# Two blocks on one NeuronCore: weight parts of the seven-product blocks prepared one product earlier, and the first FFN's input placed 448 bytes further on

## The chip, the cores and the metric

The kernel runs on one core of a Trainium2 chip. Its time is the device time of one execution in microseconds (us). A program on the core is split over five engines with a queue of instructions each: TensorE (PE, matrix products), VectorE (DVE), ScalarE (ACT), GpSimd (POOL), and SyncE (SP), which here only issues DMAs. Each queue runs in its own order and waits on semaphores for the others.

## The reference

Two transformer blocks follow each other on x of 512 tokens by 1024 features, all in float32. Only their feed-forward parts (FFN) matter here:

```
hffn = modulate(rmsnorm(x, g_norm2[l]), shift2, scale2)
a, u = jnp.split(jnp.einsum('bsd,df->bsf', hffn, w_ffn_in[l]), 2, axis=-1)
x = x + gate2[:, None, :] * jnp.einsum('bsf,fd->bsd', jax.nn.silu(a) * u, w_ffn_out[l])
...
h = rmsnorm_2(x, norm_ffn[l])
x = x + (jax.nn.silu(h @ w_ffn_gate[l]) * (h @ w_ffn_up[l])) @ w_ffn_down[l]
```

The hidden width is 2816, which is 22 tiles of 128. The rest (an adaptive norm, stick-breaking attention, retention, sparse attention with a learned index, gated linear attention) is the same in both kernels.

## The kernel before

Activations lie with features on the partitions and the 512 tokens along the row. Every float32 operand is split into a high part, rounded to `fp32r`, and a low part (the rest), and a product of tiles is three matmuls, high by high, low weight by high, high weight by low (L1800, L1802, L1805, 512 columns each). Weights come in blocks of 1024 by 256 into one of three buffers `stg` (SP), ScalarE rounds the high part into `wh`, and VectorE or GpSimd subtracts it for the low part `wl`. There are six slots of 128 by 512 in each of `wh` and `wl`.

Both FFNs ("a" is the first, "b" the second) compute most of their gate and up columns in another way, which saves an eighth of the products: a weight block (2 by 2 halves) and the input (2 by 2 halves) are multiplied in seven products instead of eight, with sums of the parts as operands (the method of Strassen and Winograd). A product `(g, m)` is product m of block g. It is 12 matmuls of 256 columns, four times L1830 (high by high), L1832 (low weight `wl`) and L1834 (low input). Products 1, 2 and 3 read the input itself, `hH`/`hL` in FFN a and `h2H`/`h2L` in FFN b; products 4 to 7 read sums of it, `tHa`/`tLa` and `tHb`/`tLb`. Each FFN does this in two lots of ten blocks, gate and up in turn, with the products onto the output width behind each lot. Before the first lot's blocks stand four ordinary jobs of 512 columns on the same input (96 matmuls in all).

The weights of products 1, 2 and 4 are corners of the block, straight from `stg`; their low parts are made by GpSimd (L3086). Those of products 3, 5, 6, 7 are sums of corners, S4, S1, S2, S3, which VectorE writes into PSUM (L2321; S1, named `bank<-stg`, reads two corners in SBUF, S4 is `bank<-stg,bank_pair`, S3 `bank_pair<-stg,bank_pair`, S2 `bank_pair<-bank,stg`), and their low parts VectorE makes too (L2327). ScalarE makes all high parts (L2828) in the order of the products. After a product, `part` adds it to what belongs to it: VectorE after products 1, 6 and 7 (L2343), ScalarE after 2, 3 and 5 (L2840). After product 4 and product 6 a finished row of the block is multiplied, put through silu, split (`row_mult`, `row_silu`, `row_scale`, `row_high`, `row_low`): VectorE L2353/L2355 or L2359/L2361 and L2089, GpSimd L3095, L3099, L3110, L3021. FFN b scales both blocks' rows by the norm's factor, so GpSimd has eleven operations in 14 products there, and eight in FFN a.

The order of products is the list `items`. In the steady state, with block g and the next one n, it is (n,5), (g,6), (n,2), (n,3), (g,7), (n,1), (g,4). `fast` writes out every engine's order around it: before product i, `before(i)` first emits the low parts whose high parts the last call emitted (`lows`), then the sums that are due and whose places are free, and then prepares the next items as far as a limit on `state["next"]` allows, where `quad_high` is emitted and the low part is left for the next call. After the product come its `part` and the row steps that are due. A slot can be written once the product six slots back is done. A block's `stg` buffer is loaded anew when its last low part (product 4) and last sum are done. Whatever the code emits, each engine runs it in that order.

Of the kernel before, what the change touches and what calls it, by code (L numbers as in the profile page):

```python
# [9 lines left out]
F32R = mybir.dt.float32r  # L10
# [3 lines left out]
P = 128  # L14
S = 512
D = 1024
KT = D // P
# [269 lines left out]
def make_plan():  # L287
    p = Plan()
# [412 lines left out]
    def ffn(tag, x, wa, wu, u0, wd, lo):  # L701
# [65 lines left out]
        def fast(lot, groups, lead, tail):  # L767
# [19 lines left out]
            state = {"next": 1, "open": False}  # L787
# [36 lines left out]
            def before(i):  # L824

                while lows:
                    low(*lows.pop(0))
                due.extend(sums.get(i, ()))
                while due and ready(*due[0]):
                    add(*due.pop(0))  # L830
                while state["next"] < len(items):
                    item = items[state["next"]]
                    if isinstance(item, int) and item < p.ahead:
                        state["next"] += 1
                        continue
                    if isinstance(item, int):
                        u = len(p.units) + len(p.units) % 2
                        if state["next"] > i + 3 or not (p.done(u - 6) and p.done(u - 5)):
                            return
                        p.prepare(item)  # L840
                    else:
                        g, m = item
                        if state["next"] > i + (4 if i < len(lead) and not lot else 3 if m in (1, 2, 4, 5) else 2) or not p.done(len(p.units) - 6):
                            return
                        if m in (3, 5, 6, 7) and (g, {5: 1, 6: 2, 7: 3, 3: 4}[m]) not in p.summed:
                            return
                        for b in range(p.groups[g]["b"], p.groups[g]["b"] + 3):
                            p.load(b)
                        p.quads[g, m] = {"u": len(p.units)}
                        p.units.append(("quad", g, m))  # L850
                        p.n_hi += 1
                        p.quads[g, m]["hi"] = p.n_hi
                        emit("quad_high", g, m)
                        lows.append((g, m))
                    state["next"] += 1
# [75 lines left out]
        for lot, (f0, nf) in enumerate(((0, FA), (FA, FT - FA))):  # L931
# [24 lines left out]
            if groups:  # L956
                start = last - len(groups) - 2
                lead = [start, start + 1]
# [392 lines left out]
def program(nc, a, out, scratch):  # L1351
    p = make_plan()
# [4 lines left out]
    def sb(name, shape, dt=F32, ctx=base):  # L1357
        return ctx.enter_context(nc.sbuf_tensor(name, shape, dt))

    with base:  # L1360
# [15 lines left out]
        small = sb("small", [P, 320])  # L1376
        sb("place_h", [P, 16])
        XR = sb("XR", [P, KT, S])
        hH = sb("hH", [P, KT, S], F32R)
        hL = sb("hL", [P, KT, S], F32R)  # L1380
        SQ = sb("SQ", [P, S])
        MEAN = {n: matf[:, i, :] for i, n in enumerate((D, 512, P))}
        RT = SQ
# [113 lines left out]
        def operand(x, k):  # L1497

            what = x[0] if isinstance(x, tuple) else x
            if what == "os":  # L1500
                return osH[:, k, :], osL[:, k, :]
            if x == ("or", 3):
                return or3H[:, k, :], or3L[:, k, :]
            if what == "or":
                return orH[:, k, :], orL[:, k, :]
            if what == "h4" and k >= 4:
                return goH[:, k - 4, :], goL[:, k - 4, :]
            if what == "mg":
                return mH[:, k, :], mL[:, k, :]
            if what == "h5":  # L1510
                return h2H[:, k, :], h2L[:, k, :]
            if what == "fa":
                return fHa[:, k, :], fLa[:, k, :]
            if what == "fb" and k >= KT:
                return fHb[:, k - KT, :], fLb[:, k - KT, :]
            return hH[:, k, :], hL[:, k, :]
# [1685 lines left out]
```

## Time and profile before

| | |
|---|---|
| median of 3 runs | 1801.43 us (1801.07 to 1806.17) |
| the profiled execution | 1803.78 us, of which 1802.0 us from the first to the last instruction (span) |
| mean granted TensorE clock | 0.997 |
| FFN a, product blocks | from about 841 to 939 us, and 1005 to 1107 us |
| FFN b, product blocks | from 1464 to 1562 us, and 1627 to 1731 us |

The profile is of one execution. In its timeline a row is one instruction (or a run of like ones): start, duration, engine, line, what it writes and reads. TensorE's matmuls overlap: one lasts 0.28 us, and the next begins 0.11 to 0.12 us after it, so the time of a product is the distance between the first matmul of it and that of the next. A wait can therefore hide in a matmul that lasts longer, and the idle time of PE is less than what a late operand costs.

### The profile page before, as it was taken

The numbers are of one execution on the slowest core, as the hardware profiler recorded it, in microseconds if no ns is written. First come the engines' busy times: TensorE is split into PE (matmuls) and PEld (weight loads), VectorE is DVE, ScalarE is ACT, GpSimd is POOL, SyncE is SP. The second block draws the span as 40 slices with busy tenths as digits, with TensorE's granted clock in tenths as the row PEclk, the third lists the DMA queues.
The fourth block names the chain that finished last, engine by engine and source line by source line (L and its number), as shares of the span: only waits on it lengthen the run. The fifth ranks groups of instructions, "written<-read, shape, count | busy, mean of one in ns | idle before, by whom it ended". The sixth has DMA issues, their size and how long they took to land.

```text
span 1802.0 us, 25394 instructions
## 1 busy us (share of the span) xinstructions
PE 1774.3 (98%) x9960; PEld 1468.2 (81%) x9960; DVE 962.6 (53%) x1600; ACT 804.8 (45%) x1355; POOL 794.7 (44%) x607
## 2 busy tenths in 40 slices
PE   9999999999999999999999999999999999999997
PEld 7777778878778787887998899777776789888986
DVE  7567541434151303338764465648777677635754
ACT  5555551233233323437552354535546565424542
POOL 5444345546365534432540243144556347505740
PEclk9999999999999999999999999999999999999999
DMA  9321223545443122422533233432222123232322
GB/s 355 119 70 48 71 71 116 177 147 174 147 140 105 60 93 71 140 94 73 152 95 116 72 117 97 116 98 83 92 80 76 47 71 111 93 125 71 114 92 76
DMA packets 158872, 192.12 MB, mean 107 GB/s; under 512 B 10345, under 2 KB 141689, under 8 KB 158370
## 3 DMA queue, kind: packets, MB, share of 16 engines
q1 hardware_dynamic: 156898, 181.77, 31.2%
q0 software_dynamic: 1104, 5.24, 0.9%
q10 hardware_dynamic: 752, 3.49, 0.5%
q8 instruction: 80, 1.31, 0.3%
q14 instruction: 38, 0.31, 0.1%
HBM read 188.37 MB, written 4.72 MB: 107 GB/s over the span
## 4 chain that ended last, share of the span: by engine, by line
PE 91%; DVE 6%; issue 2%; ACT 1%; DMA 0%; POOL 0%; DVEq 0%; ACTq 0%
PE bank L1800 19%; PE bank L1805 19%; PE bank L1802 19%; PE bank L1832 6%; PE bank L1834 6%; PE bank L1830 6%; PE bank L1909 2%; DVE wl L2327 1%; PE bank L1843 1%; PE bank_pair L1805 1%; PE bank_pair L1802 1%; PE bank_pair L1800 1%; PE bank_pair L1859 1%; DVE left L2164 1%; PE bank L1879 1%
## 5 line engine op out<-in xcount | busy, mean ns | idle before, releaser
L1800 PE MATMUL bank<-hH,wh 128*128 128x512 f32 x1040 | 424.8, 408 | 0.0
L3030 POOL TENSOR_TENSOR wl<-stg,wh 128x512 fp32r<-128x512 f32 x150 | 202.6, 1351 | 475.1 <-ACT wh L2639 474.9
L1805 PE MATMUL bank<-hL,wh 128*128 128x512 f32 x1040 | 406.4, 391 | 0.0
L1802 PE MATMUL bank<-hH,wl 128*128 128x512 f32 x1040 | 405.8, 390 | 0.0
L2639 ACT ACTIVATE wh<-stg 128x1024 fp32r<-128x1024 f32 (+2 forms) x222 | 216.6, 978 | 217.4 <-PE bank L1805 168.4
L3086 POOL TENSOR_TENSOR wl<-stg,wh 128x512 fp32r<-128x512 f32 x120 | 165.7, 1390 | 196.0 <-ACT wh L2828 195.7
L1800 PEld LDWEIGHTS bank<-hH,wh 128*128 128x128 f32 x1040 | 195.4, 188 | 56.6 <-issue 19.7
L1805 PEld LDWEIGHTS bank<-hL,wh 128*128 128x128 f32 x1040 | 195.2, 188 | 42.3
L1802 PEld LDWEIGHTS bank<-hH,wl 128*128 128x128 f32 x1040 | 195.7, 188 | 39.3 <-issue 2.9
L3031 POOL TENSOR_TENSOR wl<-stg,wh 128x512 fp32r<-128x512 f32 x150 | 204.8, 1366 | 0.0
L2343 DVE TENSOR_TENSOR tmps<-bank,tmps 128x256 f32<-128x256 f32 x120 | 50.8, 424 | 111.0 <-PE bank L1834 111.0
L2840 ACT ACTIVATE tmps<-bank 128x256 f32<-128x256 f32 x120 | 45.9, 384 | 143.7 <-PE bank L1834 143.4
L2121 DVE TENSOR_TENSOR wl<-stg,wh 128x768 fp32r<-128x768 f32 (+2 forms) x72 | 75.9, 1060 | 61.8 <-ACT wh L2639 61.4
L2134 DVE CUSTOM_DVE_ANT_0 stg<-stg,cb,col 128x1024 f32<-128x1024 f32 x32 | 55.7, 1775 | 79.8 <-DMA stg<-in_w_ada_t 79.8
L1832 PE MATMUL bank<-tHb,wl 128*128 128x256 f32 x320 | 90.5, 283 | 2.5 <-DVE wl L2327 1.7
L1832 PE MATMUL bank<-tHa,wl 128*128 128x256 f32 x320 | 89.8, 281 | 2.2 <-DVE wl L2327 1.7
L1830 PE MATMUL bank<-tHb,wh 128*128 128x256 f32 x320 | 88.8, 278 | 2.2 <-DVE tmps L2343 2.2
L1830 PE MATMUL bank<-tHa,wh 128*128 128x256 f32 x320 | 89.1, 278 | 1.4 <-DVE tmps L2343 1.4
L1834 PE MATMUL bank<-tLa,wh 128*128 128x256 f32 x320 | 88.7, 277 | 0.0
L1834 PE MATMUL bank<-tLb,wh 128*128 128x256 f32 x320 | 88.7, 277 | 0.0
L2828 ACT ACTIVATE wh<-stg 128x512 fp32r<-128x512 f32 x120 | 75.7, 631 | 11.5 <-PE bank L1805 11.5
L1832 PE MATMUL bank<-hH,wl 128*128 128x256 f32 x240 | 68.4, 285 | 1.4 <-DVE wl L2327 1.4
(394 smaller groups left out, 4065.7 us busy)
## 6 DMA issues: line engine op xcount, KB each, us to landing
stg<-in_w_in SPq DMA_DIRECT2D x54, 1024.0 KB, 5.2
stg<-in_w_ada_t SPq DMA_DIRECT2D x48, 512.0 KB, 4.7
stg<-in_w_ffn_in SPq DMA_DIRECT2D x22, 1024.0 KB, 5.1
stg<-in_w_ffn_gate SPq DMA_DIRECT2D x11, 1024.0 KB, 5.3
stg<-in_w_ffn_up SPq DMA_DIRECT2D x11, 1024.0 KB, 5.4
stg<-in_w_proj_ret SPq DMA_DIRECT2D x8, 1024.0 KB, 5.1
stg<-in_w_out SPq DMA_DIRECT2D x8, 1024.0 KB, 5.6
stg<-in_w_ffn_out SPq DMA_DIRECT2D x8, 768.0 KB, 4.9
```

The lines of the kernel that those rows point to most:

```text
L1800: T.matmul(ps, wh, xh, start=j["first"] and k == 0, stop=False)
L1802: T.matmul(ps, wl, xh, start=False, stop=False)
L1805: t = T.matmul(ps, wh, xl, start=False, stop=j["stop"] and last)
L1830: T.matmul(ps, wh[:, k, :], xh, start=k == 0 and m in (1, 2, 5), stop=False, skip_group_check=True)
L1832: T.matmul(ps, wl[:, k, :], xh, start=False, stop=False, skip_group_check=True)
L1834: t = T.matmul(ps, wh[:, k, :], xl, start=False, stop=k == KT // 2 - 1, skip_group_check=True)
L2121: V.tensor_tensor(lo, src, hi, ALU.subtract).then_inc(s["w_lo_dve"], 1)
L2639: A_.activation(hi, src, ACTF.Copy).then_inc(s["w_hi"], 1)
L2828: A_.activation(hi, src, ACTF.Copy).then_inc(s["w_hi"], 1)
L3030: G.tensor_tensor(lo[:, 0:h, :], src[:, 0:h, :], hi[:, 0:h, :], ALU.subtract)
L3031: G.tensor_tensor(lo[:, h:, :], src[:, h:, :], hi[:, h:, :], ALU.subtract).then_inc(s["w_lo_pool"], 1)
L3086: G.tensor_tensor(lo, src, hi, ALU.subtract).then_inc(s["w_lo_pool"], 1)
```

## The change

Two edits. The first is in the limit on how far ahead items may be prepared: products 1, 2, 4, 5 at most four items ahead instead of three, products 3, 6, 7 three instead of two (four for all in the lead of a first lot, as before). When the sums are made doesn't change in the code.

The second makes `hH` and `hL` one allocation with 128 more columns. All users but one keep their addresses. The first FFN's input (`"hn2"`) is now written and read 112 columns, 448 bytes, further on. From `hH` at byte 103040 of a partition the input moves to 103488: 128 bytes past a multiple of 512 before, 64 bytes past one now, as `h2H` (138304), `tHa` (143424) and `tHb` (171072) were. Everything allocated behind moves by 512 bytes, and keeps its place relative to 512.

```diff
-                        if state["next"] > i + (4 if i < len(lead) and not lot else 3 if m in (1, 2, 4, 5) else 2) or not p.done(len(p.units) - 6):
+                        if state["next"] > i + (4 if m in (1, 2, 4, 5) or i < len(lead) and not lot else 3) or not p.done(len(p.units) - 6):
...
-        hH = sb("hH", [P, KT, S], F32R)
-        hL = sb("hL", [P, KT, S], F32R)
+        hHL = sb("hHL", [P, 2 * KT * S + 128], F32R)
+        hH, hL = (hHL[:, i * KT * S:(i + 1) * KT * S].rearrange("p (k s) -> p k s", k=KT) for i in range(2))
+        nH, nL = (hHL[:, i * KT * S + 112:(i + 1) * KT * S + 112].rearrange("p (k s) -> p k s", k=KT) for i in range(2))
...
+            if what == "hn2":
+                return nH[:, k, :], nL[:, k, :]
```

Lines behind the second edit have numbers higher by three in the changed kernel. TensorE's and SP's instructions keep their order. On VectorE in FFN b, from the `row_mult` of an up block on (gate block g, next block n), the kernel before has: the low part of (g,6), S4 of n, S3 of g, `part` after (g,6), `row_low`, the low parts of (n,3) and (g,7), S1 of the block after n, `part` after (g,7), and a low part of product 5:

```order
L2353 TENSOR_TENSOR tmps<-bank,tmps 128x256
L2355 TENSOR_TENSOR tmps<-tmps 128x256
L2327 TENSOR_TENSOR wl<-bank_pair,wh 128x512
L2321 TENSOR_TENSOR bank<-stg,bank_pair 128x512
L2321 TENSOR_TENSOR bank_pair<-stg,bank_pair 128x512
L2343 TENSOR_TENSOR tmps<-bank,tmps 128x256
L2089 TENSOR_TENSOR hL<-tmps,hH 128x512
L2327 TENSOR_TENSOR wl<-bank,wh 128x512
L2327 TENSOR_TENSOR wl<-bank_pair,wh 128x512
L2321 TENSOR_TENSOR bank<-stg 128x512
L2343 TENSOR_TENSOR tmps<-bank,tmps 128x256
L2327 TENSOR_TENSOR wl<-bank,wh 128x512
```

The same stretch of VectorE in the changed kernel:

```order
L2356 TENSOR_TENSOR tmps<-bank,tmps 128x256
L2358 TENSOR_TENSOR tmps<-tmps 128x256
L2324 TENSOR_TENSOR bank<-stg,bank_pair 128x512
L2330 TENSOR_TENSOR wl<-bank,wh 128x512
L2324 TENSOR_TENSOR bank_pair<-stg,bank_pair 128x512
L2346 TENSOR_TENSOR tmps<-bank,tmps 128x256
L2092 TENSOR_TENSOR hHL<-tmps,hHL 128x512
L2330 TENSOR_TENSOR wl<-bank_pair,wh 128x512
L2324 TENSOR_TENSOR bank<-stg 128x512
L2330 TENSOR_TENSOR wl<-bank,wh 128x512
L2346 TENSOR_TENSOR tmps<-bank,tmps 128x256 x2
L2330 TENSOR_TENSOR wl<-bank_pair,wh 128x512
```

The low part of (g,6) now stands ahead of the `row_mult` (out of sight here), that of (n,3) has moved from behind S3 and `row_low` to between S4 and S3, and that of the next product 5 from behind to ahead of the `part` after (g,7).

On GpSimd in FFN b, from one `row_low` (L3021) to the next, two blocks of the kernel before (L3099 is `row_mult` of the gate block, L3095 that of the up block, L3110 `row_scale`, L3086 low parts of products 2, 1, 4 in turn):

```order
L3021 TENSOR_TENSOR hL<-tmps,hH 128x512
L3086 TENSOR_TENSOR wl<-stg,wh 128x512
L3099 TENSOR_TENSOR tmps<-tmps,SQ 128x512
L3086 TENSOR_TENSOR wl<-stg,wh 128x512 x2
L3110 TENSOR_TENSOR tmps<-tmps,SQ 128x512
L3086 TENSOR_TENSOR wl<-stg,wh 128x512
L3110 TENSOR_TENSOR tmps<-tmps,SQ 128x512
L3095 TENSOR_TENSOR tmps<-tmps 128x512
L3086 TENSOR_TENSOR wl<-stg,wh 128x512 x2
L3021 TENSOR_TENSOR hL<-tmps,hH 128x512
```

And in the changed kernel:

```order
L3024 TENSOR_TENSOR hHL<-tmps,hHL 128x512
L3089 TENSOR_TENSOR wl<-stg,wh 128x512 x2
L3102 TENSOR_TENSOR tmps<-tmps,SQ 128x512
L3089 TENSOR_TENSOR wl<-stg,wh 128x512
L3113 TENSOR_TENSOR tmps<-tmps,SQ 128x512
L3089 TENSOR_TENSOR wl<-stg,wh 128x512
L3113 TENSOR_TENSOR tmps<-tmps,SQ 128x512
L3089 TENSOR_TENSOR wl<-stg,wh 128x512
L3098 TENSOR_TENSOR tmps<-tmps 128x512
L3089 TENSOR_TENSOR wl<-stg,wh 128x512
L3024 TENSOR_TENSOR hHL<-tmps,hHL 128x512
```

In both blocks the low part of the next block's product 1 has moved ahead of `row_mult`, which now stands between it and the low part of product 4. ScalarE's order moves in step: the high part of each product is emitted one product earlier, as far as its sum is there.

## Rows read from the trace of the kernel before

**Rows 1.** The page, busy time of each engine (share of the span), instructions.

```profile
PE 1774.3 (98%) x9960; PEld 1468.2 (81%) x9960; DVE 962.6 (53%) x1600; ACT 804.8 (45%) x1355; POOL 794.7 (44%) x607
```

**Rows 2.** Waits of PE: for whom, us in total, times, longest.

```profile
PE bank L1832 <- DVE wl L2327: 6.6, 20, 1.3
```

**Rows 3.** Groups of matmuls by form: count, then busy us, mean ns of one.

```profile
L1830 PE MATMUL bank<-hH,wh 128*128 128x256 f32 x240 | 67.6, 282 | 0.0
...
L1802 PE MATMUL bank<-h2H,wl 128*128 128x512 f32 x32 | 12.6, 395 | 0.0
...
L1802 PE MATMUL bank<-fHa,wl 128*128 128x512 f32 x132 | 51.4, 389 | 0.0
```

**Rows 4.** Timeline of PE, first matmuls of products, FFN a, then FFN b.

```profile
845.64 0.28 PE L1830 MATMUL bank<-hH,wh 128*128 128x256 f32 x1
...
847.08 0.29 PE L1830 MATMUL bank<-tHa,wh 128*128 128x256 f32 x1
...
1467.09 0.28 PE L1830 MATMUL bank<-h2H,wh 128*128 128x256 f32 x1
...
1468.45 0.28 PE L1830 MATMUL bank<-h2H,wh 128*128 128x256 f32 x1
```

**Rows 5.** Timeline of PE, FFN b, two blocks (24 gate, 25 up).

```profile
1506.70 0.28 PE L1830 MATMUL bank<-h2H,wh 128*128 128x256 f32 x1
...
1509.42 0.28 PE L1830 MATMUL bank<-tHb,wh 128*128 128x256 f32 x1
...
1510.78 0.28 PE L1830 MATMUL bank<-tHb,wh 128*128 128x256 f32 x1
1511.13 0.39 PE L1832 MATMUL bank<-tHb,wl 128*128 128x256 f32 x1
...
1519.84 0.28 PE L1830 MATMUL bank<-tHb,wh 128*128 128x256 f32 x1
...
1526.97 0.28 PE L1830 MATMUL bank<-h2H,wh 128*128 128x256 f32 x1
```

**Rows 6.** Timeline of VectorE in the same stretch.

```profile
1509.72 0.42 DVE L2353 TENSOR_TENSOR tmps<-bank,tmps 128x256 f32<-128x256 f32 x1 [0.43 <-PE bank L1834]
1510.06 0.42 DVE L2355 TENSOR_TENSOR tmps<-tmps 128x256 f32<-128x256 f32 x1
...
1510.99 0.69 DVE L2321 TENSOR_TENSOR bank<-stg,bank_pair 128x512 f32<-128x512 f32 x1
1511.59 0.69 DVE L2321 TENSOR_TENSOR bank_pair<-stg,bank_pair 128x512 f32<-128x512 f32 x1
1512.70 0.43 DVE L2343 TENSOR_TENSOR tmps<-bank,tmps 128x256 f32<-128x256 f32 x1 [0.42 <-PE bank L1834]
...
1514.84 1.83 DVE L2321 TENSOR_TENSOR bank<-stg 128x512 f32<-128x512 f32 x1
```

**Rows 7.** Timeline of ScalarE in the same stretch.

```profile
1512.31 0.60 ACT L2828 ACTIVATE wh<-bank_pair 128x512 fp32r<-128x512 f32 x1
1512.80 0.62 ACT L2828 ACTIVATE wh<-stg 128x512 fp32r<-128x512 f32 x1
```

**Rows 8.** Timeline of GpSimd in the same stretch.

```profile
1513.20 1.66 POOL L3099 TENSOR_TENSOR tmps<-tmps,SQ 128x512 f32<-128x512 f32 x1 [3.08 <-DVE tmps L2343]
1514.82 3.00 POOL L3086 TENSOR_TENSOR wl<-stg,wh 128x512 fp32r<-128x512 f32 x2
1517.78 1.30 POOL L3110 TENSOR_TENSOR tmps<-tmps,SQ 128x512 f32<-128x512 f32 x1
```

**Rows 9.** The page, DMA issues: count, KB, us from issue to landing.

```profile
stg<-in_w_ffn_gate SPq DMA_DIRECT2D x11, 1024.0 KB, 5.3
```

**Rows 10.** Timeline of PE, FFN a, two blocks: first matmuls 14 products apart.

```profile
883.41 0.28 PE L1830 MATMUL bank<-hH,wh 128*128 128x256 f32 x1
...
903.71 0.28 PE L1830 MATMUL bank<-hH,wh 128*128 128x256 f32 x1
```

**Rows 11.** Timeline of VectorE, FFN a, S1 of block 3.

```profile
863.29 3.15 DVE L2321 TENSOR_TENSOR bank<-stg 128x512 f32<-128x512 f32 x1 [1.89 <-DMA stg<-in_w_ffn_in]
```

## The prediction, as it went on record

> **What bounds the kernel now.** I read the page's busy shares first: PE is busy 98% of the span, VectorE 53%, ScalarE 45%, GpSimd 44% [rows 1]. So only PE's own time counts, or what makes PE late. The waits of PE say how late: 6.6 us in 20 waits for low parts from VectorE [rows 2]. That understates it, since a waiting matmul looks long. In the timeline of PE a product with its operands there takes 1.36 us (1467.09 to 1468.45); one on the first FFN's input takes 1.44 (845.64 to 847.08) [rows 4]. Against that two blocks of FFN b, fourteen products, take 20.27 us (1506.70 to 1526.97) [rows 5] where 14 x 1.36 is 19.04: 1.23 us are lost per pair of blocks. In FFN a a pair takes 20.30 [rows 10]; six of its products read the input at 0.08 more each, so 0.78 are lost. One loss is seen whole: product (24,6) begins at 1510.78 and its first `wl` matmul only at 1511.13, 0.35 later instead of 0.11 [rows 5].
>
> The cause is an order. The low part of (24,6) stands on VectorE behind the `row_mult` of block 23 (1509.72, 1510.06) [rows 6], which waits for product (23,4) to end at 1509.42 [rows 5]. The low part of the next product 3 stands likewise behind `part` and `row_low`.
>
> **Part 1, the placement.** 60 products of FFN a read the input (240 matmuls of one kind, four in a product [rows 3]). At 64 bytes past a multiple of 512 they should take the 1.36 us of `h2H`, which lies so, instead of 1.44 [rows 4]: 60 x 0.08 = 4.8 us less. The same place costs the ordinary 512-column jobs something: 395 ns on `h2H` against 389 on `fHa`, which lies 128 past [rows 3]; 96 x 6 ns = 0.6 more. Net -4.2 us. Bounds: 0, if the 0.08 belongs to something else about that input, and -4.8.
>
> The Trainium skill ("TensorE: Matmul & The Clock Gate", "Back-to-back issue gap") puts the gap at the columns over 2.4 GHz plus 2.5 ns, 109 ns at 256 columns as an estimate, whatever the address. The trace shows 113 and 120 on like matmuls at one clock [rows 4], and by the page alone part 1 would be worth 0.
>
> **Part 2, the order.** Nothing is added or removed; three things move. I take the end of product (g-1,4) as zero (1509.42 in the rows) and follow the gate block of a pair in FFN b, with durations from the three engines' timelines [rows 6 to 8]: a 512-wide VectorE operation holds its queue 0.60 and is done after 0.69, a 256-wide one 0.34 and 0.42; ScalarE 0.49 and 0.60; GpSimd 1.26 and 1.30 (1514.82 + 3.00 is 1517.82, the next begins at 1517.78). VectorE starts `row_mult` 0.30 after the product's end (1509.42 to 1509.72); other handovers I take as 0.04 to 0.08, as from 1512.70 + 0.43 to 1513.20.
>
> Before: `row_mult` 0.30, S4 at 1.57, S3 at 2.17 [rows 6], high part of (g,7) 2.89, of (n,1) 3.38 to 4.00 [rows 7]. GpSimd did `row_mult` at 3.78 (1.66 long), then the low parts of (n,1) and (g,4), 5.40 to 8.40 [rows 8]. (g,4) begins six products later, at 8.16 without a stall.
>
> After: the low part of (g,6) is long made, so PE's stalls there go (the gain). `row_mult` waits 0.08 for S2 and runs to 1.04; S4 1.04 to 1.73. Now the low part of (n,3) stands between S4 and S3, and needs its high part first: ScalarE 1.77 to 2.36, VectorE 2.40 to 3.08, VectorE idle for 0.75 in front of it. S3 thus runs 3.00 to 3.69 instead of 2.17 to 2.86. High part of (g,7) 3.73, of (n,1) 4.21 to 4.84. GpSimd has the low part of (n,1) first in its queue now, so it idles until 4.92 although `row_mult` could start at about 4.1, and is done at 6.21. VectorE meanwhile does `part` (3.60), `row_low` (3.95), the low part of (g,7) (4.55 to 5.23, PE wants it at 5.55: no stall), and comes to S1 of the block after n at 5.15.
>
> S1 reads two tensors in SBUF, and so does every GpSimd operation here. The rows show what happens when they meet [rows 6, 8]: S1 at 1514.84 took 1.83 us instead of 0.69 beside a GpSimd operation begun at 1514.82, and the two GpSimd operations took 3.00 together instead of 2.55. The Trainium skill ("SBUF — State Buffer", "SBUF: two separate sides") has this as an exclusive lock on a shared port pair, held for a whole instruction, against VectorE operations with two SBUF inputs; the trace agrees with these numbers.
>
> So S1 waits to 6.21 and ends at 6.77; GpSimd's `row_mult` runs from there to 8.06 and the low part of (g,4) to 9.33. PE gets it at 9.39 and wants it at 8.16 + 0.11 = 8.27: a stall of 1.12 and 0.11 for the restart (as where the matmul behind a stalled one is late too [rows 5]). The half pair lasts 10.75 us, where it lasted 10.42 (1509.42 to 1519.84) [rows 5].
>
> The up block's half goes the same way from its zero: `row_mult`'s second half meets a GpSimd low part (0.34 lost), S4 1.30 to 1.99, low part of product 3 to 3.34, S3 3.26 to 3.95, high part of product 1 to 5.10, GpSimd low part 5.18 to 6.46, S1 to 7.02, `row_mult` to 8.28, low part of product 4 to 9.58: PE is late by 1.37, the half lasts 11.0 where it lasted 20.27 - 10.42 = 9.85. With the same meeting in the next gate half (0.25) a pair takes 22.0: 1.7 more than before. Ten blocks are five pairs in a lot, the first one only partly in this state, so nine pairs in two lots: +15 us. None of the busy shares [rows 1] shows such a limit, since the engines of this chain take turns.
>
> FFN a has no `row_scale`, and `row_mult` on GpSimd for up blocks alone. Gate half: GpSimd's low part of (g,4) is done by 8.06, in time. But the low part of the next product 5 stands ahead of the `part` after (g,7): S1 ends 6.77, high part 7.41, low part begins 7.44, `part` 8.04 to 8.47, and product (g,4), which adds to that result, begins at 8.52 instead of 8.16. With the restart 0.47, up to 0.7 where `row_mult` met GpSimd. Up half 0.1 to 0.2. A pair loses about 0.9 instead of 0.78: +1 us over nine pairs. Bounds for it: -7 (nothing is late any more), +12 (below).
>
> SP's queue keeps its order; a `stg` load waits for the low part of product 4, at 9.33 behind zero, and takes 5.3 us [rows 9], so it lands at about 14.7. Its first reader is the S1 in the next half, at about 10.75 + 5.2 = 15.9: hidden, by 1.2 us. If that cover went, VectorE would stand still as it once did in FFN a [rows 11].
>
> **Sum.** -4.2 + 15 + 1 = +12 (11.8) on the profiled execution's 1803.8 us: 1815.6. That execution is 2.4 above the median of the three runs, so 1813 us in their terms.
>
> **Rivals.**
>
> *Faster: the stalls vanish and nothing replaces them.* For it: the only operands that PE waits for steadily are VectorE's low parts, and these do come earlier; no engine is near its limit. Then FFN b gives back 9 x 1.23 = 11 us, FFN a 9 x 0.78 = 7, with the placement 22: 1779. The deciding point is whether GpSimd's low part of product 4 is ready 8.2 us after zero. Against: even in the order before it was ready only at 8.40 (1517.82) [rows 8], and had slack only since PE had stalled earlier. If just one step of my chain failed, the meeting of S1 with GpSimd, the stall in the gate half would still be 0.6. Half of this rival lies near 1787. Chance 0.22.
>
> *Nothing but the placement counts.* The new stalls weigh as much as the old ones, in FFN b too: 1797 to 1807. It needs S3's delay of 0.8 us and GpSimd's new order to cost half of what I found. Chance 0.15.
>
> *Worse: S1 loses the port twice.* In one place S1 took 3.15 us [rows 11], since a second GpSimd operation went ahead of it. In FFN a that would put `part` after (g,7) another 1.3 us late in each pair, +12: 1825. Elsewhere it lost once only [rows 6]. Chance 0.07.
>
> *The placement gives nothing*, the rest as forecast: 1817, inside the forecast's own range.
>
> **How the numbers follow.** The forecast has a chance of 0.56, with its own range of 1807 to 1822 (FFN b from +9 to +20, FFN a from -1 to +4, placement -4.8 to 0). What 0.3% of this kernel is, 5.4 us, is about what a measurement tells from no change. Faster 0.22 (the first rival), same 0.15 (the second), slower 0.63 (forecast and double loss). The range of 1790 to 1822 leaves out the far part of the first rival (0.14) and the double loss (0.06).
>
> **What would show it.** The products on the first FFN's input 1.36 us apart. In FFN b first matmuls 14 products apart by 21.5 to 22 us; the stalls of products 6 and 3 gone, and in their place idle time of PE in front of the `wl` matmul of product 4, released by GpSimd's low part (L3089), twice per pair; S1 on VectorE (L2324) longer than 1 us in most pairs; VectorE idle before the low part of product 3, released by ScalarE. In FFN a short waits for the `part` after product 7. The forecast is wrong if GpSimd's low part of product 4 comes before PE: then a pair in FFN b would be shorter than 20.27.

## The result and the profile after

The changed kernel takes 1817.98 us (median of 4 runs, 1815.0 to 1819.78); the kernel before, run beside it, 1803.16 (4 runs). The ratio is 1.0075, with a 95% interval of 1.0063 to 1.0087: 11 to 16 us slower. The profiled execution has a span of 1816.6 us, 14.6 more than before. The page's busy shares (engine, us, share of the span, instructions) and its chain by engine:

```profile
PE 1779.4 (98%) x9960; PEld 1470.8 (81%) x9960; DVE 1000.4 (55%) x1600; ACT 805.1 (44%) x1355; POOL 795.2 (44%) x607
...
PE 80%; POOL 6%; DVE 6%; issue 5%; ACT 2%; DMA 0%; DVEq 0%; ACTq 0%; POOLq 0%
```

The shares hardly differ from those of before [rows 1]. VectorE is busy 38 us longer with the same 1600 instructions, so some of them got longer. The waits of PE (for whom; us in total, times, longest) show where it waits now:

```profile
PE bank L1833 <- DVE tmps L2346: 13.1, 20, 2.9
PE bank L1835 <- POOL wl L3089: 4.3, 14, 0.3
PE bank L1835 <- DVE wl L2330: 2.6, 2, 1.3
```

Of the kernel before, the second line of the view from which [rows 2] shows the first:

```profile
PE bank L1830 <- DVE tmps L2343: 3.7, 3, 1.4
```

The 20 waits for low parts from VectorE [rows 2] have become 2. The waits for `tmps`, which is the `part` behind product 7 that product 4 adds to, have grown from 3 to 20, and 14 for low parts from GpSimd are new. Timeline of PE in FFN b, at three products 4 and at the end of the first of them (start, us; in brackets the idle time before and its releaser):

```profile
1510.95 0.38 PE L1833 MATMUL bank<-tHb,wh 128*128 128x256 f32 x1 [0.43 <-DVE tmps L2346]
1511.64 0.38 PE L1835 MATMUL bank<-tHb,wl 128*128 128x256 f32 x1 [0.31 <-POOL wl L3089]
...
1513.02 0.28 PE L1833 MATMUL bank<-tHb,wh 128*128 128x256 f32 x1
...
1521.75 0.38 PE L1833 MATMUL bank<-tHb,wh 128*128 128x256 f32 x1 [0.34 <-DVE tmps L2346]
1522.44 0.38 PE L1835 MATMUL bank<-tHb,wl 128*128 128x256 f32 x1 [0.31 <-POOL wl L3089]
...
1532.55 0.38 PE L1833 MATMUL bank<-tHb,wh 128*128 128x256 f32 x1 [0.42 <-DVE tmps L2346]
```

Both half pairs, one block each, last 10.80 us (1510.95, 1521.75, 1532.55), the pair 21.60, where it lasted 20.27 [rows 5]. Product 4 waits twice: in front of its first matmul, and in front of its first `wl` matmul. The second wait decides, since the low part lands at the same time however early the first matmul went.

Now the chain behind it. Zero is the end of product 4, taken as 1513.02, where the first matmul of the next product begins. VectorE's timeline:

```profile
1513.32 0.42 DVE L2356 TENSOR_TENSOR tmps<-bank,tmps 128x256 f32<-128x256 f32 x1 [0.48 <-PE bank L1837]
...
1514.29 0.68 DVE L2324 TENSOR_TENSOR bank<-stg,bank_pair 128x512 f32<-128x512 f32 x1
1515.64 0.69 DVE L2330 TENSOR_TENSOR wl<-bank,wh 128x512 fp32r<-128x512 f32 x1 [0.67 <-ACT wh L2831]
1516.25 0.69 DVE L2324 TENSOR_TENSOR bank_pair<-stg,bank_pair 128x512 f32<-128x512 f32 x1
...
1518.38 1.63 DVE L2324 TENSOR_TENSOR bank<-stg 128x512 f32<-128x512 f32 x1
1520.67 0.69 DVE L2330 TENSOR_TENSOR wl<-bank,wh 128x512 fp32r<-128x512 f32 x1 [0.67 <-ACT wh L2831]
1521.28 0.74 DVE L2346 TENSOR_TENSOR tmps<-bank,tmps 128x256 f32<-128x256 f32 x2
```

These are `row_mult`, S4, the low part of product 3 with VectorE idle 0.67 in front of it, S3 at 3.23, S1 (1.63 us instead of 0.69), the low part of the next product 5, and the `part` for which PE waits. GpSimd's timeline goes with it:

```profile
1518.16 1.29 POOL L3089 TENSOR_TENSOR wl<-stg,wh 128x512 fp32r<-128x512 f32 x1 [4.08 <-ACT wh L2831]
1519.41 1.74 POOL L3102 TENSOR_TENSOR tmps<-tmps,SQ 128x512 f32<-128x512 f32 x1
1521.11 1.28 POOL L3089 TENSOR_TENSOR wl<-stg,wh 128x512 fp32r<-128x512 f32 x1
```

GpSimd idles 4.08 us, makes the low part of product 1, then `row_mult`, and the low part of product 4 until 1522.39, which is 9.37 behind zero. Over the whole first lot of FFN b VectorE's groups (count, then busy us, mean ns, idle before) say the same of nearly every block: S1 took 910 ns in the mean before and takes 1625 now, and the waits for ScalarE's high part in front of a low part were 0.0 before.

```profile
L2324 DVE TENSOR_TENSOR bank<-stg 128x512 f32<-128x512 f32 x9 | 14.6, 1625 | 0.1
L2330 DVE TENSOR_TENSOR wl<-bank_pair,wh 128x512 fp32r<-128x512 f32 x20 | 13.8, 688 | 3.7 <-ACT wh L2831 3.7
L2330 DVE TENSOR_TENSOR wl<-bank,wh 128x512 fp32r<-128x512 f32 x19 | 13.1, 691 | 12.0 <-ACT wh L2831 12.0
```

Where the difference adds up is seen in the timeline of PE, from the first matmul of the first product to that of the last in each lot of seventy products. For FFN b's first lot that is 1584.15 - 1464.34 = 119.81 us after and 1577.21 - 1464.37 = 112.84 before; for its second 124.36 after and 116.64 before. FFN b is 14.7 us longer. FFN a is 2.9 shorter: 112.20 and 114.49 in its two lots instead of 113.95 and 115.67. Together +11.8. The remaining 2.8 of the span lie ahead of the first product of FFN a (844.29 against 841.36). Of them 2.7 are there at the 61st matmul (19.11 against 16.45), in the loads at the start. In the traces of this document FFN a's first product begins between 840.4 and 842.0 (seven of them) or between 844.2 and 844.8 (the other seven), with and without the placement and the order, so I count it as scatter of single executions.

### The profile page after: what moved, and what is told of

Read it like the earlier page. It is cut to its first block, busy times and chain, and to the rows that moved or that the text cites. A ratio compares the mean times of both kernels' runs of the same rounds, so it can differ in the third digit from the quotient of the medians.

```text
span 1816.6 us, 25422 instructions
## 1 busy us (share of the span) xinstructions
PE 1779.4 (98%) x9960; PEld 1470.8 (81%) x9960; DVE 1000.4 (55%) x1600; ACT 805.1 (44%) x1355; POOL 795.2 (44%) x607
## 3 DMA queue, kind: packets, MB, share of 16 engines
q8 instruction: 80, 1.31, 0.3%
## 4 chain that ended last, share of the span: by engine, by line
PE 80%; POOL 6%; DVE 6%; issue 5%; ACT 2%; DMA 0%; DVEq 0%; ACTq 0%; POOLq 0%
PE bank L1803 19%; PE bank L1808 18%; PE bank L1805 18%; POOL wl L3089 3%; PE bank L1835 2%; PE bank L1833 2%; PE bank L1837 2%; PE bank L1912 2%; DVE bank L2324 1%; PE bank L1846 1%; POOL tmps L3098 1%; PE bank_pair L1803 1%; PE bank_pair L1805 1%; PE bank_pair L1808 1%; PE bank_pair L1862 1%
## 5 line engine op out<-in xcount | busy, mean ns | idle before, releaser
L1803 PE MATMUL bank<-hHL,wh 128*128 128x512 f32 x1040 | 425.4, 409 | 0.0
L3033 POOL TENSOR_TENSOR wl<-stg,wh 128x512 fp32r<-128x512 f32 x150 | 202.7, 1351 | 473.6 <-ACT wh L2642 473.4
L1808 PE MATMUL bank<-hHL,wh 128*128 128x512 f32 x1040 | 406.9, 391 | 0.0
L1805 PE MATMUL bank<-hHL,wl 128*128 128x512 f32 x1040 | 406.4, 391 | 0.0
L3089 POOL TENSOR_TENSOR wl<-stg,wh 128x512 fp32r<-128x512 f32 x120 | 159.3, 1331 | 265.4 <-ACT wh L2831 265.3
L1803 PEld LDWEIGHTS bank<-hHL,wh 128*128 128x128 f32 x1040 | 195.8, 188 | 56.9 <-issue 19.7
L1808 PEld LDWEIGHTS bank<-hHL,wh 128*128 128x128 f32 x1040 | 195.5, 188 | 42.5
L1805 PEld LDWEIGHTS bank<-hHL,wl 128*128 128x128 f32 x1040 | 196.0, 188 | 39.2 <-issue 2.9
L3034 POOL TENSOR_TENSOR wl<-stg,wh 128x512 fp32r<-128x512 f32 x150 | 204.9, 1366 | 0.0
L2831 ACT ACTIVATE wh<-bank 128x512 fp32r<-128x512 f32 x80 | 47.9, 598 | 145.5 <-DVE bank L2324 133.0
L2330 DVE TENSOR_TENSOR wl<-bank,wh 128x512 fp32r<-128x512 f32 x80 | 55.3, 691 | 48.3 <-ACT wh L2831 48.2
L2831 ACT ACTIVATE wh<-stg 128x512 fp32r<-128x512 f32 x120 | 71.3, 625 | 11.5 <-PE bank L1808 11.5
L1833 PEld LDWEIGHTS bank<-tHb,wh 128*128 128x128 f32 x320 | 60.4, 189 | 13.7 <-DVE tmps L2346 13.3
```

Source lines behind the costliest of these rows:

```text
L1803: T.matmul(ps, wh, xh, start=j["first"] and k == 0, stop=False)
L1805: T.matmul(ps, wl, xh, start=False, stop=False)
L1808: t = T.matmul(ps, wh, xl, start=False, stop=j["stop"] and last)
L1833: T.matmul(ps, wh[:, k, :], xh, start=k == 0 and m in (1, 2, 5), stop=False, skip_group_check=True)
L2831: A_.activation(hi, src, ACTF.Copy).then_inc(s["w_hi"], 1)
L3033: G.tensor_tensor(lo[:, 0:h, :], src[:, 0:h, :], hi[:, 0:h, :], ALU.subtract)
```

## The experiments

Stage lengths are in us, worked out as above, both lots added, each from one execution. A pair is the distance of first matmuls 14 products apart, from one block's product 4 to the one two blocks on, in the steady part of FFN b. The ratio is to the kernel before, run beside it. FFN b of the changed kernel, e2 and e5 holds 1.6 us each of a lower granted clock, of which more below. e10 and e11, with one run each, stand at the end.

| kernel | ratio (95%) | FFN a | FFN b | pair in FFN b |
|---|---|---|---|---|
| before | 1 | 229.6 | 229.5 | 20.27 |
| changed | 1.0075 (1.0063 to 1.0087) | 226.7 | 244.2 | 21.6 |
| e1, placement alone | 0.9982 (0.9973 to 0.9991) | 226.5 | 229.4 | 20.25 |
| e2, order alone | 1.0080 (1.0066 to 1.0093) | 228.0 | 244.1 | 21.6 |
| e3, low part 3 behind row_low | 0.9988 (0.9979 to 0.9996) | 224.2 | 232.1 | 20.53 |
| e4, low part 1 behind row_mult | 0.9985 (0.9976 to 0.9993) | 222.9 | 232.0 | 20.6 to 20.8 |
| e5, S1 with one operand in SBUF | 1.0029 (1.0018 to 1.0040) | 224.4 | 237.2 | 20.73 |
| e6, both moved | 0.9994 (0.9985 to 1.0003) | 223.6 | 232.4 | 20.5 to 20.8 |
| e7, low part 3 directly behind S3 | 0.9967 (0.9955 to 0.9980) | 220.9 | 227.7 | 20.0 to 20.2 |
| e8, look-ahead for 3, 6, 7 only | 0.9987 (0.9977 to 0.9998) | 220.7 | 231.3 | 20.75 |
| e9, part, then low part 3 | 0.9953 (0.9939 to 0.9968) | 217.3 | 230.1 | 20.70 |
| e12, e9 with a row_scale on VectorE | 0.9955 (0.9941 to 0.9968) | 219.1 | 228.2 | 20.4 to 20.5 |

### e1 and e2: each part alone

e1 keeps the buffer `hHL` and its views and takes the condition on the look-ahead back; e2 is the reverse:

```diff
-                        if state["next"] > i + (4 if m in (1, 2, 4, 5) or i < len(lead) and not lot else 3) or not p.done(len(p.units) - 6):
+                        if state["next"] > i + (4 if i < len(lead) and not lot else 3 if m in (1, 2, 4, 5) else 2) or not p.done(len(p.units) - 6):
```

> The placement alone, the order of before kept. My theory: the products on the first FFN's input take 1.36 us as those on the second FFN's do, FFN b's pairs stay at 20.27 us, and the kernel is 4 us faster than before (1799, ratio 0.998). Rival (the later start of the first product in the changed kernel, 844.3 us against 841.4, comes from the placement): the first product of FFN a still begins near 844 and the gain is 1 to 2 us or nothing.

> The further look-ahead alone, the input at its old place. My theory: pairs of FFN b at 21.6 us, FFN a's pairs about 0.5 longer than in the changed kernel (20.4 to 20.8), the kernel 17 to 18 us slower than before (ratio 1.0095 to 1.010). If it and the placement add up, the two ratios times each other give the 1.0075 of the changed kernel. Rival (the placement causes part of the loss, through the engines that read the input in other places): pairs of FFN b below 21.4.

Placement alone: 1.6 to 4.9 us faster by the ratio, 3.1 in FFN a's stages, nothing in FFN b. Its first product begins at 841.86, so the late start isn't the placement's. Order alone: 1.0080, a little less than the 1.0095 expected; FFN b is 14.6 us longer, as in the changed kernel, but FFN a's pairs, expected at 20.4 to 20.8, take 19.8 to 20.1 in their steady part. The two ratios times each other are 1.0062, which the intervals of all three allow. Within them the parts add up, and the loss is the order's, in FFN b.

### e3 and e4: one operation moved back

In both, a low part gets the index of the product from which it may be made; in e3 product 3's waits one product longer, in e4 product 1's (`m == 1`).

```diff
-                while lows:
-                    low(*lows.pop(0))
+                for x in [x for x in lows if x[2] <= i]:
+                    lows.remove(x)
+                    low(*x[:2])
...
-                        lows.append((g, m))
+                        lows.append((g, m, i + (2 if m == 3 else 1)))
```

> The changed kernel with one operation moved on VectorE: the low part of product 3 stands behind S3, part and row_low, not between S4 and S3. My theory: VectorE no longer idles 0.67 us in front of S3; S3, the high part of product 1, S1 and all behind them come 0.7 us earlier, product 4 stalls by about 0.5 instead of 1.15, pairs of FFN b take 20.1 to 20.4 instead of 21.6, the kernel 10 to 13 us faster than the changed one (1805 to 1808). Rival (only GpSimd's own queue, with the low part of product 1 ahead of row_mult, makes the low part of product 4 late): pairs stay within 0.3 of 21.6.

> The changed kernel with one operation moved on GpSimd: the low part of product 1 stands behind row_mult, as before the change, and nothing else moves. My theory: row_mult starts at about 4.1 us behind the end of product 4 instead of 6.4, the low part of product 4 is done at 7.9 to 8.4 instead of 9.37, and what is left is the wait of product 4 for the part behind product 7, about 0.5: pairs of FFN b at 20.2 to 20.6, the kernel 9 to 12 us faster than the changed one. Rival (only VectorE's idle time in front of S3 counts): pairs stay within 0.3 of 21.6.

Either move takes the new loss away: pairs of 20.53 and 20.6 to 20.8 instead of 21.6. Both rivals, each of which needed one engine's order alone, fall. The chain is one in series, and 0.7 us off it at VectorE or a reordering at GpSimd is enough. But e3 stops 0.1 and e4 up to 0.2 short of what I expected, and both stay above the 20.27 of before. With either move the pair is left with other waits. Timeline of PE in e3:

```profile
1502.79 0.39 PE L1836 MATMUL bank<-tHb,wl 128*128 128x256 f32 x1 [0.40 <-POOL wl L3090]
...
1509.03 0.38 PE L1836 MATMUL bank<-h2H,wl 128*128 128x256 f32 x1 [0.52 <-DVE wl L2331]
```

and in e4:

```profile
1504.62 0.39 PE L1836 MATMUL bank<-h2H,wl 128*128 128x256 f32 x1 [0.57 <-POOL wl L3090]
...
1514.99 0.38 PE L1836 MATMUL bank<-h2H,wl 128*128 128x256 f32 x1 [0.57 <-POOL wl L3090]
```

What is left in e3 is product 4 once per pair and product 3 once. In e4 it isn't the `part` behind product 7, as I had expected: PE waits for the low part of product 1, which now stands behind `row_mult`, in both halves. The kernels are faster than I expected, since FFN a and the ends of the lots gained too.

### e5: S1 without its second operand in SBUF

```diff
-                    x, y, op = corner(g, 1, 2), corner(g, 2, 2), ALU.add
+                    x, y, op = corner(g, 1, 2), sum_of(g, 1), ALU.add
```

> The changed kernel, but S1 takes its second operand from its own bank in PSUM and no longer from SBUF, so the weights of products 5, 6, 7 and 3 are not the reference's; order, shapes and waits stay. My theory: S1 (512 wide) runs 0.6 to 0.8 us in every block beside GpSimd's low part of product 1, where it took 1.6 to 1.8; GpSimd's row_mult behind it takes 1.3 instead of 1.74; product 4 finds its part in time and its own low part 0.45 us earlier: pairs of FFN b at 20.6 to 20.9 instead of 21.6, the kernel 7 to 9 us faster than the changed one. Rival (the meeting only shows in S1's record, and the wait on GpSimd's queue decides alone): S1 gets short and the pairs stay at 21.5 or more.

What S1 adds is then whatever lies in its bank, so the kernel leaves out the right sum and keeps the order, the shapes and the waits.

VectorE's groups in the first lot of FFN b, S1's row:

```profile
L2324 DVE TENSOR_TENSOR bank<-stg,bank 128x512 f32<-128x512 f32 x9 | 6.2, 686 | 0.1
```

GpSimd's timeline in one gate block:

```profile
1514.61 1.30 POOL L3089 TENSOR_TENSOR wl<-stg,wh 128x512 fp32r<-128x512 f32 x1 [4.08 <-ACT wh L2831]
1515.86 1.31 POOL L3102 TENSOR_TENSOR tmps<-tmps,SQ 128x512 f32<-128x512 f32 x1
```

S1 runs at 686 ns in all nine blocks, and `row_mult` behind the low part at 1.31 instead of 1.74. The pair is 20.73 and the kernel 1.0029 against 1.0075: 8.3 us (0.0046 times 1803), as expected. So the meeting of S1 with GpSimd is worth 0.9 of the 1.3 us that a pair lost. The Trainium skill ("SBUF — State Buffer", "SBUF: two separate sides") names, beside VectorE's 2-port modes, operations with two inputs in SBUF as those that an exclusive lock sets against GpSimd. This run agrees, since with one of the two in PSUM nothing was held up beside the same GpSimd operations.

### e6 and e7: both moved, and the low part of product 3 in two places

e6 has `m in (1, 3)` in e3's edit. e7 delays product 1's alone and lets the low part of product 3 follow S3 at once:

```diff
+                due.extend(sums.get(i, ()))
+                for x in [x for x in lows if x[2] <= i]:
+                    if x[1] == 3 and due and due[0][1] == 3:
+                        while due and ready(*due[0]):
+                            add(*due.pop(0))
+                    lows.remove(x)
+                    low(*x[:2])
```

> The changed kernel with both moves: the low part of product 3 behind row_low on VectorE, that of product 1 behind row_mult on GpSimd. My theory: product 4 and product 1 find their operands in time (row_mult from 3.5 us behind the end of product 4, the low parts of products 1 and 4 done near 6.3 and 7.6, wanted at 6.9 and 8.3). What is left is the wait for the low part of product 3, some 0.3 to 0.5, since it stands behind row_low. Pairs of FFN b at 19.4 to 20.0, the kernel 1788 to 1795. Rival (each move alone had taken away the same wait, and another limit near 20.5 us per pair holds, for example buffers that PE frees too late): pairs stay at 20.4 to 20.7.

> As the run with both moves, but the low part of product 3 stands directly behind S3 on VectorE, ahead of part and row_low. My theory: now no operand is late in the steady state; pairs of FFN b near 19.1 to 19.4 (19.04 is fourteen times 1.36), FFN a's near 19.1 to 19.5, the kernel 1780 to 1788. If S3's follower row_low gets late instead, the first matmul of nothing waits for it. Rival (a limit near 20.5 us per pair that no order of these two operations moves): pairs stay at 20.4 or more.

I was wrong on e6: the two moves don't add up, and its ratio is that of no change. GpSimd's low part of product 1 is late in one half, VectorE's of product 3 in the other. e7 is better, 0.9967, but its pairs of 20.0 to 20.2 are not the 19.1 to 19.4 expected, nor its 1796.6 us the 1780 to 1788. VectorE's and GpSimd's timelines in e7, one gate block:

```profile
1507.47 0.69 DVE L2334 TENSOR_TENSOR wl<-bank,wh 128x512 fp32r<-128x512 f32 x1
1508.08 0.41 DVE L2350 TENSOR_TENSOR tmps<-bank,tmps 128x256 f32<-128x256 f32 x1
```

```profile
1508.57 1.68 POOL L3106 TENSOR_TENSOR tmps<-tmps,SQ 128x512 f32<-128x512 f32 x1 [2.66 <-DVE tmps L2350]
1510.22 2.99 POOL L3093 TENSOR_TENSOR wl<-stg,wh 128x512 fp32r<-128x512 f32 x2
```

The `part` behind product 6 now follows the low part of product 3 without a gap, so the low part delays it, and with it `row_mult` and the low part of product 1. In FFN a, which has less on GpSimd, pairs fell to 19.0 to 19.3 in the first lot, as expected; in the second they take 19.79 without any wait, which the last section takes up.

### e8: further look-ahead for VectorE's products alone

```diff
-                        if state["next"] > i + (4 if m in (1, 2, 4, 5) or i < len(lead) and not lot else 3) or not p.done(len(p.units) - 6):
+                        if state["next"] > i + (4 if i < len(lead) and not lot else 3) or not p.done(len(p.units) - 6):
```

> The changed kernel with the further look-ahead only for products 3, 6 and 7, whose low parts VectorE makes; products 1, 2, 4 and 5 as before. VectorE's order is that of the changed kernel near S3, GpSimd's that of before. My theory: like the run with row_mult first, a wait of about 0.5 to 0.6 for GpSimd's low part of product 1 in each half, pairs of FFN b at 20.5 to 20.9, the kernel at 1799 to 1803. Rival (the idle time on VectorE in front of S3 makes product 4 late by itself): pairs above 21.2.

Pairs in FFN b of 20.75, as in e4, and 1799.7 us: as expected. FFN a has no steady wait (19.04 in the first lot). With GpSimd's order of before, VectorE's idle time in front of S3 does no harm.

### e9: the part first, then the low part of product 3

e6's edit, and in `product`, behind `emit("part", g, m)`:

```diff
+                    for x in [x for x in lows if m == 6 and x[1] == 3]:
+                        lows.remove(x)
+                        low(*x[:2])
```

> As the run with the low part of product 3 directly behind S3, but on VectorE the part behind product 6 stands between the two: S3, part, low part of product 3, row_low. What the runs so far showed: with the low part ahead of the part, the part ran 0.4 us later and with it GpSimd's row_mult and the low part of product 1, for which PE waited 0.4 (pairs 20.1); with it behind row_low PE waited 0.5 for the low part of product 3 (20.5). My theory (each of these operations is late by its place in a queue alone): neither is late now, pairs of FFN b at 19.0 to 19.9, the kernel 1786 to 1793. Rival (GpSimd's own work, 1.7 + 3.0 us behind the part in each gate half, is the limit): pairs stay at 20.0 or more.

The kernel is at 0.9953 (1794.3 us, just beyond the 1793 expected), but it got there by FFN a, where the steady pairs of the second lot are 19.04. In FFN b the rival held: 20.70. The gate half has lost its wait for product 1; the up half has not. Timeline of PE, then of GpSimd, in the up half:

```profile
1518.90 0.38 PE L1839 MATMUL bank<-h2H,wl 128*128 128x256 f32 x1 [0.50 <-POOL wl L3093]
```

```profile
1514.54 1.30 POOL L3117 TENSOR_TENSOR tmps<-tmps,SQ 128x512 f32<-128x512 f32 x1 [2.39 <-ACT tmps L2856]
1515.80 1.80 POOL L3102 TENSOR_TENSOR tmps<-tmps 128x512 f32<-128x512 f32 x1
1517.57 2.52 POOL L3093 TENSOR_TENSOR wl<-stg,wh 128x512 fp32r<-128x512 f32 x2
```

GpSimd's `row_scale` of the gate block, which FFN a doesn't have, stands ahead of `row_mult`, and the low part of product 1, the first of the two in the last row, is done at 1518.84.

### e12: that row_scale on VectorE

GpSimd's `row_scale` returns at once for that row, and the semaphore it ticks is VectorE's; these lines are left out here.

```diff
+            def row_scale(g, row):
+                if row == 1:
+                    return
+                dst = row_of(g, row)
+                ticked(ve, "silu", g, row)
+                V.tensor_tensor(dst[:, :], dst[:, :], RT[:, :], ALU.mult).then_inc(s["v_f"], 1)
```

> As the run with the part ahead of the low part of product 3, but in FFN b the second row_scale of each gate block is made by VectorE, at the same place in the program, and not by GpSimd. In the run before, the half of the up block lost 1.2 us per pair: PE waited 0.67 for GpSimd's low part of product 1, behind row_scale 1.3, row_mult 1.8 and the meetings with VectorE. Theory (GpSimd's own work in this half is the limit that is left): row_mult starts 1.2 us earlier there, this wait goes, a smaller one of 0.3 to 0.5 for VectorE's low part of product 7 may come, since row_scale reads two tensors in SBUF beside row_mult; pairs of FFN b at 19.6 to 20.3 instead of 20.7, the kernel 1786 to 1792. Rival (any work put on VectorE costs there what it saves on GpSimd, because the two take turns at SBUF): pairs at 20.5 or more.

The pairs, 20.4 to 20.5, lie between the two expectations, and the ratio doesn't differ from e9's. Timeline of VectorE and PE:

```profile
1514.27 1.41 DVE L2357 TENSOR_TENSOR tmps<-tmps,SQ 128x512 f32<-128x512 f32 x1
```

```profile
1516.33 0.38 PE L1839 MATMUL bank<-tHb,wl 128*128 128x256 f32 x1 [0.21 <-DVE wl L2334]
```

The wait for product 1 is gone, and a wait for VectorE's low part of product 7 is in its place, because the moved operation reads two tensors in SBUF, meets `row_mult` and takes 1.41 us instead of 0.69. Relieving GpSimd bought 0.2 to 0.3 us a pair. How low FFN b can go with another division of this work stays open.

### e10 and e11: other places for the input

The placement alone, with 96 elements (0 bytes past a multiple of 512) in e10 and 16 (192 bytes past) in e11 instead of 112:

```diff
-        nH, nL = (hHL[:, i * KT * S + 112:(i + 1) * KT * S + 112].rearrange("p (k s) -> p k s", k=KT) for i in range(2))
+        nH, nL = (hHL[:, i * KT * S + 96:(i + 1) * KT * S + 96].rearrange("p (k s) -> p k s", k=KT) for i in range(2))
```

> The placement alone, with the input at a multiple of 512 bytes instead of 64 past one. Theory (any place but 128 past a multiple is as good): its products take 1.36 us, or 1.41 where PE keeps its slower pace, as in the run of the placement alone. Rival (the place must be 64 past a multiple, like the other operands'): 1.44 as before the change, or another length of its own.

> The placement alone, with the input 192 bytes past a multiple of 512, so 64 past a multiple of 128 as in the changed kernel. Theory (only the remainder by 128 counts): products on it 1.36 to 1.41 us. Rival (the remainder by 512 counts and each has its own length): 1.44 or more.

Both had one run, 1805.99 and 1799.96 us, which tells nothing at this size; the length of a product in the trace does. First matmuls of products that follow each other, in e10:

```profile
883.24 0.28 PE L1833 MATMUL bank<-hHL,wh 128*128 128x256 f32 x1
...
884.67 0.28 PE L1833 MATMUL bank<-hHL,wh 128*128 128x256 f32 x1
```

and in e11:

```profile
879.07 0.28 PE L1833 MATMUL bank<-hHL,wh 128*128 128x256 f32 x1
...
880.48 0.28 PE L1833 MATMUL bank<-hHL,wh 128*128 128x256 f32 x1
```

A product on the input takes 1.43 us at 0 past a multiple of 512, 1.44 at 128 [rows 4], 1.41 at 192 and 1.36 at 64. Other operands, all at 64, go at 1.36 between them in both traces, but for product 7 in e10, which takes 1.41 between two products on the input. So the place matters, the changed kernel has the best of the four for these products, and both simple theories fall: not every place but 128 is good, and the remainder by 128 doesn't decide. The 1.41 at 192 is also the length of a product at the slower pace of the last section; whether the two are the same thing isn't shown. For the 96 ordinary matmuls of 512 columns ahead of the first product 64 isn't the best place: they take 22.45 us at 128, 22.47 at 192, 22.80 at 0 and 22.82 to 22.84 at 64.

## Why the prediction was right, and where it was off

- **Direction and size.** 1813 us and slower was said, within 1790 to 1822; 1818 came out. The forecast's own case (slower by the order of FFN b) is the one that happened. The sum said +11.8 and the ratio gives +13.5 (11 to 16). That the term for FFN b came out so close (+15 said, 14.7 measured) is luck, as the points on it below show.
- **Part 1, the placement.** Net -4.2 was said; e1 gives -3.2 by its ratio (-1.6 to -4.9). In FFN a's stages it is -3.1, where 4.8 was said, and the 96 ordinary matmuls ahead of them lost 0.4, where 0.6 was said. The 0.08 per product was right. But the second product 3 of each pair still waits for its low part, and lasts 1.87 to 1.89 in e1 as it did before, so its 0.08 is not gained; and some products ran at the slower pace of the last section (1.41). The bound 0 is excluded: matmuls of 256 columns came 113, 118 and 120 ns apart. The Trainium skill ("TensorE: Matmul & The Clock Gate", "Back-to-back issue gap") gives columns over 2.4 GHz plus 2.5 ns for an isolated matmul, an estimate of 109 ns here, without a term for the address; the page says itself that a stream with weight loads goes by another spacing. The measurement differs and decides.
- **The chain in the gate half.** Said and measured, behind zero: S3 at 3.00 (3.23), S1 held up until GpSimd's operation ends at 6.21 (1519.45 - 1513.02 = 6.43) and done 0.56 later (0.56: 6.99), the low part of product 4 at 9.33 (9.37), PE's `wl` matmul at 9.39 (9.42), the half pair 10.75 (10.80). e3 confirms VectorE's order, e4 GpSimd's, e5 the port, each by taking it away.
- **The term of 15 us was mis-sized.** The up half was over-priced (11.0 said, 10.80 measured), and the further 0.25 in the next gate half didn't come. So a pair costs 1.33 more, not 1.7. Nine full pairs were too many as well: up to the last gate block's product 4 the two lots lost 5.2 and 4.3 us, 9.5 together.
- **The end of each lot in FFN b was put at nothing.** Product 4 of the last gate block had waited 1.2 us for its `part` before the change and waits 2.9 now. Two of the three waits for `tmps` of before are these, 1.19 and 1.06 us; neither [rows 2] nor the forecast takes them up. Timelines around it, of PE before, then of ScalarE, VectorE and PE after:

```profile
1560.65 0.39 PE L1830 MATMUL bank<-tHb,wh 128*128 128x256 f32 x1 [1.19 <-DVE tmps L2343]
```

```profile
1563.95 0.64 ACT L2852 ACTIVATE tmps<-tmps 128x512 f32<-128x512 f32 x1 [1.58 <-POOL tmps L3102]
```

```profile
1565.35 1.85 DVE L2124 TENSOR_TENSOR wl<-stg,wh 128x768 fp32r<-128x768 f32 x1 [3.67 <-ACT wh L2642]
1567.12 0.74 DVE L2346 TENSOR_TENSOR tmps<-bank,tmps 128x256 f32<-128x256 f32 x2
```

```profile
1567.58 0.38 PE L1833 MATMUL bank<-tHb,wh 128*128 128x256 f32 x1 [2.88 <-DVE tmps L2346]
```

  `row_mult` behind a low part on GpSimd makes `silu` late, which stands ahead of the high part of the next 768-column weights, and VectorE has their low part (1.85 us) ahead of the `part`. e4 and e5 bear this out: in the first lot the wait is 0.87 us with `row_mult` first again, and still 2.88 with the port alone relieved. From one product's first matmul to the next's that is 1.7 and 1.8 us more, 3.5 in all.
- **The granted clock fell once, and no term stood for it.** Behind the second of these waits in the changed kernel the clock is 0.50 for a moment, the 1.2 GHz level, where it is 1.00 at that place before. The window (us, busy of PE, PEld, DVE, ACT, POOL, then clock, DMA share, GB/s) and two matmuls of 512 columns that follow each other there:

```profile
1744.00:1746.00 2.00, 2.00 (x9) 1.71 (x8) 0.98 (x3) 0.87 (x2) 0.00 (x0) 0.50 0.01 3
...
1745.99 0.63 PE L1803 MATMUL bank<-hHL,wh 128*128 128x512 f32 x1
1746.41 0.63 PE L1805 MATMUL bank<-hHL,wl 128*128 128x512 f32 x1
```

  They begin 0.43 us apart instead of 0.23, and the product's length with what is inserted behind it grows from 4.90 to 6.54 us: 1.6 us. The same happened once in e2 and once in e5, each time behind a wait of 2.9 us. These three traces have six such waits, of 2.7 to 2.9 us, and three falls. In the other traces the wait is 1.6 us or less, and the clock stays at 1.00 through FFN b. The three parts, 9.5, 3.5 and 1.6, are the 14.7 measured: what was left out happened to be about as large as what was too much.
- **The wait for the part behind product 7** was said for FFN a alone. It is there in FFN b too (0.43), hidden in the longer wait for the low part. e5 shortened both together. It isn't what e4 left over.
- **FFN a** was said to lose 0.9 instead of 0.78 per pair with the order alone; e2 has most pairs at 19.8 to 20.4 where 20.3 stood [rows 10], 1.6 us less for the stage. The sign was wrong there, by 2 to 3 us of 1800. S1 takes long there too (1550 ns, mean of the seven of the first lot from 860 us on in the changed kernel), but with less on GpSimd the low part of product 4 is in time.
- **The faster rival** fails where it was said to be decided, at GpSimd's low part of product 4 (9.37, wanted at 8.27). With the meeting at the port alone taken away (e5) waits of 0.40 to 0.56 were left, where 0.6 was said. The rival holds in FFN a: with the order of e8 in its first lot, and that of e9 in its second, nothing is late in the steady state and a pair takes 19.04. The loads stayed hidden in FFN b (S1's idle time before is 0.1 us in the nine blocks); in FFN a's first lot S1 waited 3.5 us for them in all, where it had waited 1.9.

## What to carry to other kernels

Preparing an operand earlier did not add work here, but it put an operation ahead of others in an in-order queue. Follow the queue to the operation that comes late for it, across engines, before crediting the stall that goes. Don't put an operation that waits for another engine's result ahead of one that feeds that engine (here the low part of product 3 ahead of S3), and look at which VectorE operation with two inputs in SBUF will start beside a GpSimd one. Steady pairs are not the whole stage: the last block before the schedule changes deserves its own chain. e9 and e12, with the new order put right at two places, are 0.3 to 0.6% faster than the kernel before.

## What the runs showed of the hardware

TensorE has two paces at full granted clock. In the stretch from 1030 to 1070 us in e9 (us, busy of PE, PEld, DVE, ACT, POOL, then the clock, DMA share, GB/s):

```profile
1030.00:1050.00 20.00, 20.00 (x179) 20.00 (x178) 14.23 (x26) 11.92 (x26) 12.18 (x10) 1.00 0.34 107
1050.00:1070.00 20.00, 20.00 (x179) 20.00 (x178) 15.04 (x27) 11.45 (x25) 12.17 (x10) 1.00 0.34 109
```

and in e7 the same stretch:

```profile
1030.00:1050.00 20.00, 20.00 (x172) 20.00 (x171) 15.31 (x26) 11.67 (x27) 11.25 (x9) 1.00 0.33 107
1050.00:1070.00 20.00, 20.00 (x172) 20.00 (x171) 15.29 (x25) 11.66 (x26) 11.24 (x9) 1.00 0.32 106
```

PE never waits in either, the clock is 1.00, the operands lie at the same places, and still there are 179 matmuls in 20 us in one and 172 in the other. These counts take in the two or three that overlap a window's edges; from start to start it is 113 ns and 118 ns. A product takes 1.36 or 1.41 us, a pair 19.04 or 19.79. In the ten traces with the input at 64 bytes past a multiple of 512 (all but before, e2, e10 and e11) no product stage changes its pace without PE being held up. The smallest such hold-up is one matmul that begins 0.17 us behind the last instead of 0.11, which the timeline does not show as idle time. At a hold-up the pace may change, in either direction, and then it holds: e7 kept the slower one through the whole second lot of FFN a, behind its first product, with no wait in it. A change that takes waits away can leave PE in it: in that lot e7 and e8 took 113.4 and 113.6 us, where e9, at the faster pace but for its start, took 110.5. What sets the pace at a restart was not found.
